# Second feed-forward stage: the order of TensorE at the start of a step

## The reference

```
def conv_ffn(h, w_up, conv_w, conv_b, w_down):
    u = h @ w_up                                   # (256, 2048) @ (2048, 2 * 5632)
    u = lax.conv_general_dilated(u, conv_w[:, None, :], ..., padding=[(CONV_WIDTH - 1, 0)], ...) + conv_b
    gate, up = jnp.split(u, 2, axis=-1)
    return (jax.nn.silu(gate) * up) @ w_down       # (256, 5632) @ (5632, 2048)
...
h = h + conv_ffn(rmsnorm(h, norm_ffn[i]), ffn_w_up[i], ffn_conv_w[i], ffn_conv_b[i], ffn_w_down[i])
```

## Time and profile before

| | |
|---|---|
| median of three runs | 2347.41 us |
| the profiled execution, its own time | 2348.14 us |
| its span, first to last instruction | 2346.3 us |
| PE busy | 2327.0 us, 99% of the span |
| DVE busy | 1737.6 us, 74% |
| ACT busy | 1189.2 us, 51% |
| main DMA queue, share of the 16 engines' time | 53.9% |
| share of the chain of waits on PE | 96% |
| mean granted clock of TensorE | 0.998 |

### The profile page before, as it was taken

The page is one execution under the profiler, slowest core; times in us unless marked ns, Lnnn a source line. Parts: engine busy times, 40 slices in busy tenths (PEclk is TensorE's granted clock), DMA queues, the critical chain, the costliest instruction groups (busy, mean ns, idle before and its releaser), DMA issues.

```text
span 2346.3 us, 34584 instructions
## 1 busy us (share of the span) xinstructions
PE 2327.0 (99%) x14112; PEld 2054.9 (88%) x14112; DVE 1737.6 (74%) x1974; ACT 1189.2 (51%) x1371; POOL 6.4 (0%) x16
## 2 busy tenths in 40 slices
PE   8999999999999999999999999999999999999998
PEld 7988999888888888888988988899888888888887
DVE  6777777877777787777966777777766777666667
ACT  6556556544444444445544444556544444444444
POOL 0000000000000000000000000000000000000000
PEclk9999999999999999999999999999999999999999
DMA  9654434665555555555554554345555555555552
GB/s 323 197 171 136 162 126 147 203 198 189 192 184 197 185 190 193 182 194 168 195 177 143 184 176 162 130 158 199 196 193 183 196 181 194 189 186 182 195 197 90
DMA packets 233311, 425.01 MB, mean 181 GB/s; under 512 B 6912, under 2 KB 48672, under 8 KB 233088
## 3 DMA queue, kind: packets, MB, share of 16 engines
q1 hardware_dynamic: 232352, 421.55, 53.9%
q0 software_dynamic: 576, 1.97, 0.3%
q10 hardware_dynamic: 288, 0.13, 0.0%
HBM read 421.53 MB, written 2.10 MB: 181 GB/s over the span
## 4 chain that ended last, share of the span: by engine, by line
PE 96%; DVE 2%; DMA 1%; SPq 1%; ACT 0%; issue 0%; ACTq 0%; DVEq 0%
PE pair L369 34%; PE pair L371 18%; PE pair L340 10%; PE pair L342 10%; PE pair L341 10%; PE pair L392 6%; PE pair L394 3%; DMA raw<-in_x_w_kv 1%; PE pair L676 1%; DVE wlo L257 0%; SPq L467 0%; PE pair L664 0%; PE pair L998 0%; PE pair L654 0%; PE pair L995 0%
## 5 line engine op out<-in xcount | busy, mean ns | idle before, releaser
L257 DVE TENSOR_TENSOR wlo<-raw,whi 128x2048 fp32r<-128x2048 f32 x394 | 900.6, 2288 | 311.2 <-ACT whi L249 310.8
L249 ACT ACTIVATE whi<-raw 128x2048 fp32r<-128x2048 f32 x394 | 753.6, 1915 | 694.8 <-PE pair L371 403.3
L369 PE MATMUL pair<-xx,whi 128*128 128x512 f32 x2880 | 1002.0, 392 | 1.2
L371 PE MATMUL pair<-xx,wlo 128*128 128x256 f32 x2880 | 805.5, 280 | 0.0
L369 PEld LDWEIGHTS pair<-xx,whi 128*128 128x128 f32 x2880 | 538.9, 187 | 124.4 <-issue 5.2
L371 PEld LDWEIGHTS pair<-xx,wlo 128*128 128x128 f32 x2880 | 544.0, 189 | 0.1
L392 PE MATMUL pair<-xx,whi 128*128 128x512 f32 x640 | 229.6, 402 | 0.0
L369 PE MATMUL pair<-oo,whi 128*128 128x512 f32 x640 | 222.6, 391 | 1.2 <-DVE h L1820 1.2
L371 PE MATMUL pair<-oo,wlo 128*128 128x256 f32 x640 | 179.2, 280 | 0.0
L394 PE MATMUL pair<-xx,wlo 128*128 128x256 f32 x640 | 178.5, 279 | 0.0
L340 PE MATMUL pair<-xx,whi 128*128 128x256 f32 x608 | 174.7, 287 | 3.8 <-DVE wlo L1603 2.6
(11 more groups left out here) (214 smaller groups left out, 3055.0 us busy)
## 6 DMA issues: line engine op xcount, KB each, us to landing
raw<-in_ffn_w_up SPq DMA_DIRECT2D x176, 1024.0 KB, 5.0
raw<-in_ffn_w_down SPq DMA_DIRECT2D x88, 1024.0 KB, 5.0
raw<-in_diff_w_qkv SPq DMA_DIRECT2D x48, 1024.0 KB, 5.2
raw<-in_swa_w_qkv SPq DMA_DIRECT2D x20, 1024.0 KB, 5.0
raw<-in_swa_w_o SPq DMA_DIRECT2D x16, 1024.0 KB, 5.0
raw<-in_diff_w_o SPq DMA_DIRECT2D x16, 1024.0 KB, 5.0
raw<-in_x_w_kv SPq DMA_DIRECT2D x15, 1024.0 KB, 9.0
raw<-in_x_w_q SPq DMA_DIRECT2D x8, 1024.0 KB, 5.3
```

The source lines that it names most:

```text
L249: act.activation(whi[:, s], raw[:, s], ACT.Copy).then_inc(hi_ready, 1)
L257: dve.tensor_tensor(wlo[:, s], raw[:, s], whi[:, s].bitcast(F32), ALU.subtract)\
L369: pe.matmul(banks[m], whi[:, s, k, w], act2[:, c].rearrange("p a t -> p (a t)"), start=c == 0, stop=False, skip_group_check=True)
L371: ins = pe.matmul(banks[m][:, 0:SEQ], wlo[:, s, k, w], act2[:, c, 0], start=False, stop=last and k == 3, skip_group_check=True)
```

## The change

It does two things, both in layer 1 only and both at the first gate unit of steps 2 to 10. The wait on `units_used` is taken out. And in that unit the pair of bank 0, chunk 1 (the second pair) is turned round: its 256-column matmul comes first and its 512-column matmul second. The same 32 matmuls are issued, into the same banks.

```diff
-        def wide_unit(pe, b4, j, banks, act2, kq, last, added=None, count=None):
+        def wide_unit(pe, b4, j, banks, act2, kq, last, added=None, count=None, turned=None):
...
                 for k in range(4):
                     w, c = slice(m * P, (m + 1) * P), 4 * kq + k
+                    if turned == (m, k):
+                        pe.matmul(banks[m][:, 0:SEQ], wlo[:, s, k, w], act2[:, c, 0], start=False,
+                                  stop=False, skip_group_check=True)
+                        ins = pe.matmul(banks[m], whi[:, s, k, w], act2[:, c].rearrange("p a t -> p (a t)"),
+                                        start=False, stop=False, skip_group_check=True)
+                        continue
                     pe.matmul(banks[m], whi[:, s, k, w], act2[:, c].rearrange("p a t -> p (a t)"),
                               start=c == 0, stop=False, skip_group_check=True)
...
                     if after_down:
                         pe.wait_ge(s["h_added"], i * 4 - (5 if l == 0 else 6))
-                        if l == 1:
-                            pe.wait_ge(units_used, b4 * 4)
-                        wide_unit(pe, b4, 0, GATE_BANKS, xx, 0, False).then_inc(units_used, 1)
+                        wide_unit(pe, b4, 0, GATE_BANKS, xx, 0, False, turned=(0, 1) if l == 1 else None)\
+                            .then_inc(units_used, 1)
```

## The result

The changed kernel takes 2351.07 us (median of 22 runs), the kernel before 2347.11 us in the same comparison (22 runs). The ratio is 1.0016, with a 95% interval of 1.001 to 1.0022: slower by 3.96 us, or 0.17%. One of the 22 runs of the changed kernel took 9477 us at a mean granted clock of 0.583, and the ratio leaves it out. The others lie from 2349.66 to 2352.46 us, all above the highest run of the kernel before (2348.96). So the difference is clear of the scatter of these runs, though still inside the 0.2% that the prediction called no change. The forecast was 2343.9 us, and its range ended at 2347.8; the range does not hold the result. Rival A, the slow pace, gave 2351.4 us.

The account below looks back on a forecast made before the run. PE's stream (TensorE busy 99%) was taken as the bound. Removing the waits gives 3.54 us, the turned pair 0, nothing becomes late: 2347.41 - 3.5 = 2343.9 us, range 2342.8 to 2347.8.

Parts of the forecast that it names:

- Rival A: Pair stream of steps 2 to 10: new entry runs slow, 353.2 not 346.7 ns a pair; +4.0 us, 2351.4 us; chance 0.16.
- Term 1: Nine step boundaries, second feed-forward stage: without the wait, three starts take 0.46 us, not 0.86 or 0.80; 3.54 us saved.
- rival B: Step boundaries: pause stays because PE's sequencer must round the loop and pass h_added and lo_ready; 2347.4 us; chance 0.04.
- Term 2: Turned pair in the first gate unit: order inside the pair changes no sum; 0, bounded by 0.3 us in all.
- Term 3: What is late next: nothing on DVE, weights, ACT or queues becomes late; every step takes 66.18 us instead of 66.58.
- The only unpaused entry that I had costed: Gate units following 256-column triples at 1603 us with no pause: 353.2 ns a pair, taken as evidence for the slow pace.
- The remark that a pause is not what makes a stream fast: 64 slow pairs from 1120.5 us (median 398) begin with a 467 ns matmul, so behind a pause like the last step's.

Follow-up runs that it names:

- e2: Kernel before with only the second pair of each first gate unit turned, steps 2 to 10, wait kept; 2354.14 us, ratio 1.0027.
- e1: Kernel before with only the wait on units_used taken out at all nine boundaries, no pair turned; 2352.11 us, ratio 1.0018.
- e3: Kernel before with the wait moved ahead of the second gate unit, 16 pairs later, no pair turned; ratio 1.0031 over eight runs.
- e7: Kernel before without the wait, one float32 matmul of 128 columns put ahead of the up half in steps 2 to 10; 2352.72 us, ratio 1.0016.
- e10: Kernel before without the wait, first gate unit of steps 2 to 10 in blocks of four 512-column, then four 256-column matmuls; 2344.20 us, ratio 0.9985.
- e4: Kernel before with the wait replaced by a float32 matmul of 128 columns that computes nothing of use; 2345.72 us, ratio 0.9992.
- e5: Kernel before with the wait replaced by a float32 matmul of 32 columns that computes nothing of use; 2345.26 us, ratio 0.9985.

## Why the prediction was wrong

**Term 1 was right.** The pause was of the wait and of nothing else. Predicted 0.46 us for the three starts, measured 0.46; the cover of the issued matmuls formed at the loop's end as said, so rival B is out. One row was misread, without effect: DVE's additions ahead of the boundary start at 1901.62, 1906.76, 1912.20 and 1917.64 us, for PA, PB, PC and PD in turn. So the sum at 1912.20 is that of PC, and the PB product had been added by 1907.98 us, 9.2 us before the boundary and not 3.8.

**Term 2 failed.** "A distance goes by the matmul in front, and the order inside the pair changes no sum: I take 0", with a bound of 0.3 us. In e2 the turned pair alone costs 6.7 us. I bounded an edit by the distances next to it, although rival A, some lines below, had the pair stream carry a state over hundreds of pairs. An edit at the place where that state is set can't be bounded by its own 0.03 us; the bound had to be 1152 pairs at 6.5 ns, 7.5 us. In the change itself the 0 came out by luck: behind an entry that is slow anyway the turned pair adds nothing (67.02 us a step, 67.03 in e1). The Trainium skill ("TensorE: Matmul & The Clock Gate", "Back-to-back issue gap") has the distance go by the matmul's own length too, with N / 2.4 + 2.5 ns as the isolated gap, by which a pair would take, as an estimate, 325 ns. The runs do not agree, with 346.7 or 353.3 ns for the same pair by how the stream was entered.

**Term 3 was right as far as it went**: nothing on DVE or ACT became late. But the sum stopped there and left the pace of the pairs at 346.7 ns without a row for the new entry. That is the step that failed: the new entry was taken for a fast one. It was slow, 353.3 ns a pair in all nine steps, which costs 7.5 us against the 3.54 us won; e1 shows that the entry without the wait does this with no pair turned.

**Rival A had the mechanism, the size and the place**: +4.0 us forecast, +3.96 measured; 67.0 us a step, 67.02 measured; median 398. It did not foresee e2. What failed is the weighing, 0.16 against 0.75. The only unpaused entry that I had costed was slow. Against it I set that the stream came from 512-column matmuls here, and that the turned pair changes the order; e1 shows that the first does not help, and e1 beside the changed kernel that the second does not either. Both were differences between the cases, not reasons with a sign. By the rows, the slow entry should have been the forecast. The remark that a pause is not what makes a stream fast was right: in e2 and in e3's last step the pairs behind a pause are slow.

**What stays open** is what in the entry decides. It is not the pause alone (e2), not a float32 matmul alone (e7 is slow behind one, the stream at 425 us is fast), not the lengths ahead of it alone (e1 and the earlier trace rows are slow behind 512 and 256 columns, e10 is fast behind 256). The offsets within the first matmuls, to some nanoseconds, are a candidate, since the slow pace is a pattern of three pairs that repeats from the entry on. No run varied these by themselves, so this is not shown.

## What to carry to other kernels

Before a wait or a pause is taken out of a busy matmul stream, look at the pace of the stream behind it, not just at the hole: 0.40 us of pause was worth less than the 0.83 us that the pairs behind it lost. When a stream can be seen at two paces in one trace, the pace belongs in the sum as a term, with the slow one assumed until an entry of the same kind is seen fast. When the entry is the trouble, try another order of the same matmuls at the entry: e10 keeps the won pause and the fast pace, with a step of 66.22 us where the forecast had 66.18.

## What the runs showed that I had not expected

One matmul pair turned round, with its wait in place, slows the next 126 pairs by 6.5 ns each (e2), in eight steps and not in the ninth. The slow pace is a pattern of three pairs that costs 20 ns more than three pairs at the fast pace. It lasted to the end of every stretch, 128 pairs at most, unless a pause (e3, loop steps) or a float32 matmul (425 us in the kernel before) ended it; the float32 matmul of e7 did not.

A float32 matmul of 32 columns costs at this place the same 0.22 us as one of 128 (e4, e5); both are issued as two loads and two matmuls.

In e3 the profiled executions (2347.99 and 2348.25 us) were about 7 us faster than the seven plain ones (median 2355.06). Whether the pace of the pairs makes this difference was not seen, since plain executions leave no trace. A trace has to be held against the plain times before it is read for such a state.
